# Norm weights loaded in the same transfer as the first piece of the transposed x

## What is computed

```python
h = x
xn = rms_norm(h, attn_norm)              # x * rsqrt(mean(x*x) + eps) * attn_norm
proj = xn @ w_in                         # 1024 x 3072: q,k,v of two groups of 8 heads
...                                      # MoBA softmax attention, stick-breaking attention
h = h + concat(rms_norm(o_m, out_norm_moba), rms_norm(o_s, out_norm_sb)) @ w_out
h = h + peer_ffn(rms_norm(h, ffn_norm))  # 16384 single-neuron experts, tables u and v
gate = sigmoid(rms_norm(h, ple_norm) @ w_ple_gate)
h = h + gate * (p @ w_ple)
```

## Time and profile before

| | |
|---|---|
| median of 3 runs | 971.63 us |
| the runs | 970.77, 971.77, 971.63 us |
| the profiled execution, its device time | 971.13 us |
| its span, first to last instruction | 969.4 us |
| outside the span | 1.73 us |
| granted TensorE clock, mean over the span | 0.999 |
| PE busy | 956.7 us, 99% of the span |

### The profile page before, as it was taken

The page is one execution under the profiler, slowest core; times in us unless marked ns, Lnnn a source line. Parts: engine busy times, 40 slices in busy tenths (PEclk is TensorE's granted clock), DMA queues, the critical chain, the costliest instruction groups (busy, mean ns, idle before and its releaser), DMA issues.

```text
span 969.4 us, 19176 instructions
## 1 busy us (share of the span) xinstructions
PE 956.7 (99%) x6222; PEld 873.2 (90%) x6222; DVE 694.1 (72%) x1389; ACT 609.8 (63%) x1034; POOL 331.6 (34%) x148
## 2 busy tenths in 40 slices
PE   8999999999999999999999999999999999999998
PEld 5987889999999999999999999888888888888877
DVE  6748763999996889888888884555555555566763
ACT  7578654356676888888888885555444555555643
POOL 0002220188887777777777774000000000000000
PEclk9999999999999999999999999999999999999999
DMA  9770453045554444444444445555566666555521
GB/s 333 268 280 1 152 212 131 2 173 174 188 180 174 168 160 159 166 158 167 157 168 157 167 154 184 200 191 188 191 234 240 237 238 238 194 189 192 189 102 44
DMA packets 46603, 172.08 MB, mean 178 GB/s; under 512 B 5187, under 2 KB 8684, under 8 KB 45036
## 3 DMA queue, kind: packets, MB, share of 16 engines
q1 hardware_dynamic: 46284, 171.40, 49.9%
q10 hardware_dynamic: 288, 0.28, 0.1%
HBM read 169.55 MB, written 2.11 MB: 177 GB/s over the span
## 4 chain that ended last, share of the span: by engine, by line
PE 91%; DVE 4%; issue 2%; DMA 2%; SPq 1%; POOL 1%; ACT 1%; DVEq 0%; POOLq 0%
PE bank L1204 14%; PE bank L1206 14%; PE bank L1205 14%; PE pair L1521 12%; PE pair L1520 12%; PE pair L1518 12%; PE pair L1479 3%; PE pair L1232 1%; PE pair L1233 1%; PE pair L1234 1%; DMA w_raw<-w_in 1%; PE bank L1232 1%; PE bank L1234 1%; PE bank L1233 1%; PE bank L1561 1%
## 5 line engine op out<-in xcount | busy, mean ns | idle before, releaser
L581 ACT ACTIVATE t_hi<-t_raw 128x1024 fp32r<-128x1024 f32 x256 | 270.2, 1056 | 164.7 <-DMA t_raw<-v_chunks 161.9
L1176 POOL TENSOR_TENSOR t_lo<-t_raw,t_hi 128x1024 fp32r<-128x1024 f32 x130 | 311.7, 2411 | 152.3 <-ACT t_hi L581 152.3
L1204 PE MATMUL bank<-xt_hi,t_hi 128*128 128x256 f32 x1024 | 290.7, 284 | 0.1
L1206 PE MATMUL bank<-xt_hi,t_lo 128*128 128x256 f32 x1024 | 290.4, 284 | 0.0
L1205 PE MATMUL bank<-xt_lo,t_hi 128*128 128x256 f32 x1024 | 290.4, 284 | 0.0
L908 DVE TENSOR_TENSOR t_lo<-t_raw,t_hi 128x1024 fp32r<-128x1024 f32 x126 | 154.4, 1226 | 136.2 <-ACT t_hi L581 135.8
L1518 PE MATMUL pair<-t_hi,g_hi 128*128 128x512 f32 x512 | 199.7, 390 | 0.1
L1521 PE MATMUL pair<-t_hi,g_lo 128*128 128x512 f32 x512 | 199.5, 390 | 0.0
L1520 PE MATMUL pair<-t_lo,g_hi 128*128 128x512 f32 x512 | 199.5, 390 | 0.0
L1204 PEld LDWEIGHTS bank<-xt_hi,t_hi 128*128 128x128 f32 x1024 | 197.0, 192 | 0.3 <-POOL t_lo L1176 0.3
L1205 PEld LDWEIGHTS bank<-xt_lo,t_hi 128*128 128x128 f32 x1024 | 197.0, 192 | 0.0
(11 more groups left out here) (270 smaller groups left out, 1298.9 us busy)
## 6 DMA issues: line engine op xcount, KB each, us to landing
t_raw<-u_chunks SPq DMA_DIRECT2D x128, 512.0 KB, 3.2
t_raw<-v_chunks SPq DMA_DIRECT2D x128, 512.0 KB, 3.2
w_raw<-w_query SPq DMA_DIRECT2D x4, 2048.0 KB, 7.8
w_raw<-w_in SPq DMA_DIRECT2D x3, 2048.0 KB, 10.5
w_raw<-w_out SPq DMA_DIRECT2D x2, 2048.0 KB, 7.7
wg_raw<-w_gate SPq DMA_DIRECT2D x8, 512.0 KB, 4.7
w_raw<-w_in SPq DMA_DIRECT2D x7, 512.0 KB, 8.4
w_raw<-w_in SPq DMA_DIRECT2D x2, 1024.0 KB, 10.5
```

Source lines behind the costliest of these rows:

```text
L581: nc.scalar.activation(t_hi[:, q % RING, :], t_raw[:, q % RING, :], ACT.Copy).then_inc(t_hi_ready, 1)
L1176: nc.gpsimd.tensor_tensor(t_lo[:, q, :], t_raw[:, q, :], t_hi[:, q, :].bitcast(f32), ALU.subtract).then_inc(t_lo_pool, 1)
L1204: mm(dst, ah, bh, start=(c == 0), stop=False)
L1206: ins = mm(dst, al, bh, start=False, stop=(c == n - 1))
```

## The change

The gains are put ahead of `x_t` in one host array: each partition's row is now 128 bytes of gains and then the 8192 bytes of x, 8320 bytes in all. In SBUF the gains' bytes are moved to stand right ahead of `xt_lo` (whose start moves up by 128 bytes), and one tile `gain_xt` spans both. ACT's first DMA now loads 128 + 2048 bytes for each partition, gains and piece 0; the second DMA, its semaphore `gain_loaded` and the wait on it are gone. The other three pieces are issued by SP as before, from the new array, with two dimensions instead of three. All else is the same.

```diff
-        sizes = dict(h=2 * D, xt_hi=DC * SEQ, xt_lo=DC * SEQ, cst=4 * P, gains=4 * DC, qkg=32, stats=192)
+        sizes = dict(h=2 * D, xt_hi=DC * SEQ, gains=4 * DC, xt_lo=DC * SEQ, cst=4 * P, qkg=32, stats=192)
...
-        gain = tile("gain", [P, 4, DC], where["gains"])
+        assert where["xt_lo"] == where["gains"] + 4 * 4 * DC
+        gain_xt = tile("gain_xt", [P, 4 * DC + DC * SEQ], where["gains"])
+        gain = gain_xt[:, 0:4 * DC].rearrange("p (k c) -> p k c", k=4)
...
-        xt_raw = tile("xt_raw", [P, DC, SEQ], where["xt_lo"])
+        xt_raw = gain_xt[:, 4 * DC:4 * DC + DC * SEQ].rearrange("p (c t) -> p c t", c=DC)
...
             for b in range(1, 4):
-                sp.dma_start(xt_raw[:, 2 * b:2 * b + 2, :], x_t[:, 2 * b:2 * b + 2, :]).then_inc(xt_loaded[b], 16)
+                cols = slice(4 * DC + 2 * SEQ * b, 4 * DC + 2 * SEQ * (b + 1))
+                sp.dma_start(xt_raw[:, 2 * b:2 * b + 2, :].rearrange("p a b -> p (a b)"), x_t[:, cols]
+                             ).then_inc(xt_loaded[b], 16)
...
-            act.dma_start(xt_raw[:, 0:2, :], x_t[:, 0:2, :]).then_inc(xt_loaded[0], 16)
-            act.dma_start(gain[:, :, :], gains).then_inc(gain_loaded, 16)
+            act.dma_start(gain_xt[:, 0:4 * DC + 2 * SEQ], x_t[:, 0:4 * DC + 2 * SEQ]).then_inc(xt_loaded[0], 16)
             nc.scalar.preload_act_table(ACT.Sqrt)
-            act.wait_ge(gain_loaded, 16)
...
-        "x_t": a["x"].reshape(SEQ, DC, P).transpose(2, 1, 0),
+        "x_t": np.concatenate([gains.reshape(P, 4 * DC), a["x"].reshape(SEQ, DC, P).transpose(2, 1, 0).reshape(P, -1)],
+                              axis=1),
```

More of the change, by code:

```diff
@@ L69, with layer_program @@
 OUT0, QUERY0, N_GROUPS = 6, 8, 12
-def layer_program(nc, x, x_t, p_t, rel_bias, bucket_onehot, consts, gains, qk_gain, w_in, w_out, w_query,
+def layer_program(nc, x, x_t, p_t, rel_bias, bucket_onehot, consts, qk_gain, w_in, w_out, w_query,
                   subkeys_t, u_chunks, v_chunks, w_gate, w_ple, out):
@@ L212, in layer_program @@
         x_loaded = [sem(f"x_loaded{tt}") for tt in range(TT)]
-        gain_loaded, xt_loaded = sem("gain_loaded"), [sem(f"xt_loaded{b}") for b in range(4)]
+        xt_loaded = [sem(f"xt_loaded{b}") for b in range(4)]
         piece_loaded = [sem(f"piece_loaded{c}") for c in range(5)]
@@ L1601 @@
     column = lambda g: g.reshape(DC, P).T
+    gains = np.stack([column(a["attn_norm"][0]),
+                      column(np.concatenate([a["out_norm_moba"][0], a["out_norm_sb"][0]])),
+                      column(a["ffn_norm"][0]), column(a["ple_norm"][0])], axis=1)
     arrays = {
         "x": a["x"].reshape(SEQ, D),
-        "x_t": a["x"].reshape(SEQ, DC, P).transpose(2, 1, 0),
+        "x_t": np.concatenate([gains.reshape(P, 4 * DC), a["x"].reshape(SEQ, DC, P).transpose(2, 1, 0).reshape(P, -1)],
+                              axis=1),
         "p_t": a["p"].reshape(SEQ, PLE // P, P).transpose(2, 1, 0),
@@ L1608 @@
         "consts": constants(),
-        "gains": np.stack([column(a["attn_norm"][0]),
-                           column(np.concatenate([a["out_norm_moba"][0], a["out_norm_sb"][0]])),
-                           column(a["ffn_norm"][0]), column(a["ple_norm"][0])], axis=1),
         "qk_gain": np.stack([np.tile(a["q_norm"][0], 2), np.tile(a["k_norm"][0], 2)], axis=1),
```

## The result

The changed kernel takes 963.14 us (5 runs, 962.66 to 963.66) against 971.63 us before, a ratio of 0.9911 with an interval of 0.9901 to 0.9921. It is 8.4 us faster by the spans of the two profiled executions, where I had forecast 0.4 us and a range that ended at 970.0 us. The prediction is wrong.

The account below looks back on a forecast made before the run. PE was taken as busy nearly throughout, its start bound by group 1's last transfer. Only the backlog's 0.2 us counted: 971.13 - 0.2 = 970.9 us for the profiled execution, a forecast median of 971.2 us, range 970.0 to 972.3 us.

Parts of the forecast that it names:

- What bounds the kernel: Whole kernel: PE busy 956.7 of 969.4 us, so the change acts only where PE waits, at the start and before group 1.
- The matmuls with xt_lo: Matmuls reading xt_lo 128 bytes further up: no effect, since 284 ns alike and v_all reads (277 ns) no slower than transposes (273 ns).
- rival 5: u stage: 1024 matmuls with xt_lo, 123 us in all, slow down; 1.6% is 1.9 us, at 2% 973.9 us; chance 0.02.
- The sign of being wrong: In the trace: matmuls with xt_lo not at 284 ns would show the prediction wrong.
- The gains' wait: Start of ACT: the joined transfer lands at 4.98 us, so ACT starts 0.57 us sooner.
- Where that lead goes: Start to group 1: lead shrinks to 0.06 us at piece 1, then zero; PE waits 0.25 us near 10 us; worth nothing.
- The backlog: DMA engines ahead of group 1's last quarter: without the gains' packets it shrinks by 0 to 0.36 us, taken as 0.2 us.
- The other layout of x_t: Transfers of x with 8320-byte pitch and 128-byte offset: taken as nothing; by the 256-byte rule an estimated 0.1 us cost.
- Rival 4: The layout hurts: x's packets cost more ahead of group 1, 972.4 us if cut in two, 974.0 us at double cost; chance 0.08.
- Rival 3: The pitch helps: x's pieces flow at the later stretch's 416 instead of 294 GB/s, 970.1 us; chance 0.10.
- The chances: Whole kernel: within 0.2% 0.89, faster by over 0.2% (below 969.5 us) 0.05, slower by over 0.2% 0.06; forecast itself 0.60.
- four of the five rivals: On the transfer: nothing at all (0.16), the lead goes through (0.04), the pitch helps (0.10), the layout hurts (0.08).

Follow-up runs that it names:

- the second experiment: The changed kernel with qkg (128 bytes) put ahead of the gains, so xt_lo stands 256 bytes up, joined transfer kept: 970.62 us, ratio 0.9994.
- The runs with the g tiles: The changed kernel with the v stage's weights g_hi and g_lo 128 bytes further up: 972.30 us; with g_lo alone: 968.91 us.

## Why the prediction was wrong, point by point

*What bounds the kernel.* "The change can only act where PE still waits" is the sentence that failed. It is right for transfers and waits. It is wrong for an edit that moves a tile of the u stage, which 1024 of 3072 matmuls in a row read: it can act on all of them while PE is busy from end to end. The step failed on "the matmuls that read `xt_lo`", put at nothing; they and their neighbours gave 7.99 of the 8.3 us. The page said PE 99% busy, and I took busy for fixed.

*The matmuls with xt_lo.* The prediction had the place (rival 5: 1024 matmuls, 123 us, 1.6% is enough) and lost it in two ways. It asked for slower alone, and gave 0.02. And the rows that were to bound it can't. 277 ns against 273 ns isn't "no slower" where 1.6% is enough to matter. And `v_all` is read in steps of 256 bytes, and the second experiment shows that an offset of 256 bytes is no offset. No two tiles of the long stages in the kernel before stand off each other within 256 bytes, so no row of that trace could bound this term, on the faster side least of all. I should have said so and kept both ends open. The sign of being wrong that the prediction named did come: these matmuls took 281 ns, not 284 ns. Also it isn't only the `xt_lo` matmuls: all three of a triple, and the gate matmuls between (120 to 118 ns, with addresses that the change doesn't touch), took up the new rhythm.

*A sign that was there.* The distances were 120 ns for 256 columns and 227 ns for 512 columns, 13 ns over the columns at 2.4 GHz. The Trainium skill (TensorE: Matmul & The Clock Gate, section "Wait — 56ns, not 53.3ns?") has back-to-back matmuls of a warm array at the columns plus about 2.5 ns. By that, the u stage had some 11 ns in each of 3072 matmuls, an estimate of 33 us, that something was taking. The trace agrees that the columns are not all of it (120 ns against their 107 ns); whether a figure for bf16 holds for these fp32r matmuls no run here shows. The same page of the Trainium skill (section "Step-by-step: what each phase is for") says that loading the next weights takes no SBUF bandwidth from the running matmul. The runs with the g tiles speak against taking this as "no influence": moving the weights alone by 128 bytes cost the stream up to 7 ns a matmul (227 to 234 ns); whether bandwidth is what it cost, they don't show.

*The gains' wait.* Right in kind: I had ACT at 4.98 us, it came at 4.90 us; PE at 7.28 us, it came at 7.19 us. The joined transfer took 4.1 us.

*Where that lead goes.* Right in kind: it shrank at piece 1 (7.07 instead of 7.50 us, with a wait of 0.23 us for the transfer), and the stall before group 1 stayed, at 1.23 us where it had been 1.31 us. But the lead was not lost at the next weight piece, as the prediction had it: ACT went on there at 8.52 instead of 8.91 us, and so the wait of PE of 0.25 us near 10 us did not come.

*The backlog.* Too small in the one pair of traces. I had taken 0.2 us of at most 0.36 us. In the changed kernel the last quarter came 0.44 us sooner:

```profile
7.22 10.22 DMA w_raw<-w_in
```

It was issued 0.09 us sooner (7.22 for 7.31 us) and was 0.36 us shorter on its way (10.22 for 10.58 us). A single pair of traces doesn't measure this, as the first matmul of group 1 differs by 0.8 us among kernels with the same transfers (20.29 to 21.11 us over the eight with two transfers, mean 20.63 us; 19.84 to 20.39 us over the six with the joined one, mean 20.13 us). The difference of the means is 0.5 us. The route is less sure than the size. ACT's queue did fall from 288 packets and 11.6% to 144 and 8.5% of the 10 us, while SP's rose from 66.1% to 70.5%:

```profile
q1 hardware_dynamic: 942, 2.26, 70.5%
q10 hardware_dynamic: 144, 0.28, 8.5%
```

That is 0.31 us less on each engine in ACT's queue, just under my 0.36 us, and 0.44 us more in SP's with no more bytes. So that the gains' packets shortened the backlog is not shown.

*The other layout of x_t.* The rule on transfers that don't start at a multiple of 256 bytes was to take 0.1 us off. Nothing of that size can be seen beside the 0.8 us by which such starts differ. Rival 4 is gone with the second experiment: with all the transfers changed, the time was 0.15% less to 0.03% more. Rival 3's 1.3 us less lie at the edge of that, but its mechanism didn't come: the stretch from 4.9 to 8.0 us moved 289 GB/s in the changed kernel and 294 GB/s before, not 416 GB/s.

```profile
4.90:8.00 3.10, 1.00 0.91 289
```

Neither could have given 8 us.

*The chances.* The forecast and four of the five rivals, and with them nearly all of the 0.89 for "within 0.2%", were about the transfer. For the transfer alone they hold: 970.62 us lies in the range, within 0.2%. For the diff as a whole they left out what the `sizes` line can gain: faster by over 0.2% had 0.05, and not for this reason.

## What to carry to other kernels

A change of the SBUF layout is a change to every instruction that reads or writes the moved tile; cost it there, even if no line of that stage is edited, and where all tiles of the trace stand alike, leave the term open on both sides. When a diff changes an order or a size of allocation next to its purpose, run the two apart: here one line of layout was 8 us and the purpose of the change 0.7 us, not told from nothing. To see it in a trace, count the matmuls of one kind in a stretch where PE is busy throughout; the busy share shows nothing.

## What the runs showed of the hardware

- The distance between matmuls that follow each other without a wait depends on where the streamed tiles and the weights stand against each other within 256 bytes. Fp32r, 256 columns: 120 ns when they stand alike, 117 to 118 ns on average with `xt_lo` 128 or 192 bytes off, and 118 to 119 ns with both streamed tiles 128 bytes off. 512 columns: 227 ns alike, 232 to 234 ns with the weights 128 bytes off.
- Offsets of `xt_lo` by 32, 64, 128 and 192 bytes all act (32 and 64 bytes only behind the interruption, in one run each), 256 bytes don't, and moving all tiles together by 128 bytes doesn't.
- PE can hold different rhythms on the same addresses: 2880 and later 2827 to 2848 ns a step with 64 bytes, 2880 and later 2807 to 2829 ns with 32 bytes; the change came with an interruption of the stream. Matmuls whose own tiles didn't move join in.
- Open: why 256 and 512 columns go opposite ways, and which offset is the best for a given stage. No run here counts the reads of SBUF themselves; that weights and stream meet at the memory is my reading of the runs in which only the weights moved, and the 234 ns of a matmul whose stream and meanwhile loaded weights stand alike don't follow from it. No kernel tried beats the changed one beyond the spread of the runs.
